# Encoder trunk on one core: four blocks of weight splits moved from VectorE to GpSimd, and the work around them put in another order

## The reference, cut to what matters

```python
def reference(x, ...):                       # x: (1, 1024, 1024), DEPTH = 2, all float32
    for l in range(DEPTH):
        h = rms_norm(x, norm_mix_g[l])
        proj = h @ w_in[l]                   # columns q, k, v (512 each), z_b (512), x_c (256)
        q, k, v, z_b, x_c = jnp.split(proj, splits, axis=-1)
        mix_a = neighbourhood_attention(q, k, v, rpb[l])       # 8 heads of 64, 8 x 16 neighbours
        mix_b = spatial_gating(z_b, ...)                       # gelu, layer norm, 128 x 128 per head
        mix_c = fourier_mix(x_c)                               # real part of a 2-D DFT per group
        mix = head_rms_norm(jnp.concatenate([mix_a, mix_b, mix_c], axis=-1), head_norm_g[l])
        x = x + mix @ w_out[l]
        h = rms_norm(x, norm_ffn_g[l])
        x = x + (jax.nn.silu(h @ w_gate[l]) * (h @ w_up[l])) @ w_down[l]
    return rms_norm(x, final_norm_g)
```

## Time and profile before

| | |
|---|---|
| runs, us | 2043.91, 2045.06, 2043.42 (median 2043.91) |
| profiled execution, us | 2043.91 |
| its span, us | 2042.1 |
| TensorE busy | 2007.0 us, 98% of the span |
| VectorE busy | 1537.9 us, 75% |
| ScalarE busy | 902.5 us, 44% |
| GpSimd busy | 208.9 us, 10% |
| mean granted clock of TensorE | 0.997 |

### The profile page before, as it was taken

The page is one execution under the profiler, slowest core; times in us unless marked ns, Lnnn a source line. Parts: engine busy times, 40 slices in busy tenths (PEclk is TensorE's granted clock), DMA queues, the critical chain, the costliest instruction groups (busy, mean ns, idle before and its releaser), DMA issues.

```text
span 2042.1 us, 28134 instructions
## 1 busy us (share of the span) xinstructions
PE 2007.0 (98%) x10156; PEld 1670.0 (82%) x10156; DVE 1537.9 (75%) x2519; ACT 902.5 (44%) x1611; POOL 208.9 (10%) x146
## 2 busy tenths in 40 slices
PE   7999899999999999999999999999999999999998
PEld 7888688888888888888898877888888888888887
DVE  7847874789877778787867488647997877878877
ACT  6453773443333333444644547634433333334443
POOL 1221133200000000000013022431000000000000
PEclk9999999999999999999999999999999999999999
DMA  6965754124333236633468667441343333383333
GB/s 236 216 165 139 230 155 140 51 93 166 125 111 106 98 111 253 200 99 97 121 193 206 160 176 234 133 133 42 102 172 130 109 100 102 109 322 105 95 97 124
DMA packets 131560, 293.70 MB, mean 144 GB/s; under 512 B 13024, under 2 KB 18016, under 8 KB 131168
## 3 DMA queue, kind: packets, MB, share of 16 engines
q1 hardware_dynamic: 105760, 242.63, 36.3%
q0 software_dynamic: 10880, 20.97, 6.1%
q10 hardware_dynamic: 14784, 28.31, 3.8%
HBM read 232.62 MB, written 59.24 MB: 143 GB/s over the span
## 4 chain that ended last, share of the span: by engine, by line
PE 90%; DVE 6%; issue 2%; ACT 1%; ACTq 0%; DMA 0%; POOL 0%; DVEq 0%
PE bank L2184 27%; PE bank L2185 27%; PE bank L2186 27%; PE bank L2386 2%; PE bank L2405 2%; PE bank L2335 2%; DVE s_lo L1429 1%; DVE t_lo L1848 0%; PE bank L2298 0%; PE bank L2427 0%; PE bank L2314 0%; PE bank L2420 0%; ACT s_hi L953 0%; ACT logits L1149 0%; DVE h_lo L1755 0%
## 5 line engine op out<-in xcount | busy, mean ns | idle before, releaser
L2184 PE MATMUL bank<-t_hi,s_hi 128*128 128x512 f32 (+1 forms) x1336 | 517.7, 388 | 0.7 <-DVE hid_cu L1961 0.4
L2185 PE MATMUL bank<-t_lo,s_hi 128*128 128x512 f32 (+1 forms) x1336 | 517.1, 387 | 0.0
L2186 PE MATMUL bank<-t_hi,s_lo 128*128 128x512 f32 (+1 forms) x1336 | 517.1, 387 | 0.0
L2184 PEld LDWEIGHTS bank<-t_hi,s_hi 128*128 128x128 f32 x1336 | 251.1, 188 | 52.4 <-DVE hid_cu L1961 1.3
L2186 PEld LDWEIGHTS bank<-t_hi,s_lo 128*128 128x128 f32 x1336 | 251.1, 188 | 50.6
L2185 PEld LDWEIGHTS bank<-t_lo,s_hi 128*128 128x128 f32 x1336 | 251.1, 188 | 50.5
L2184 PE MATMUL bank<-b_hi,s_hi 128*128 128x512 f32 x528 | 206.3, 391 | 0.1
L2186 PE MATMUL bank<-b_hi,s_lo 128*128 128x512 f32 x528 | 205.8, 390 | 0.0
L2185 PE MATMUL bank<-b_lo,s_hi 128*128 128x512 f32 x528 | 205.7, 390 | 0.0
L953 ACT ACTIVATE s_hi<-w_u 128x512 fp32r<-128x512 f32 x142 | 89.6, 631 | 233.1 <-PE bank L2186 175.8
L953 ACT ACTIVATE s_hi<-w_down 128x512 fp32r<-128x512 f32 x154 | 97.3, 632 | 200.2 <-PE bank L2186 199.3
(11 more groups left out here) (291 smaller groups left out, 3749.6 us busy)
## 6 DMA issues: line engine op xcount, KB each, us to landing
w_raw<-in_win SPq DMA_DIRECT2D x50, 512.0 KB, 6.0
w_g<-in_wg SPq DMA_DIRECT2D x44, 512.0 KB, 3.5
w_u<-in_wu SPq DMA_DIRECT2D x44, 512.0 KB, 4.4
t_raw<-hidden_t SPq DMA_DIRECT2D x88, 256.0 KB, 2.6
w_raw<-in_win POOLq DMA_DIRECT2D x40, 512.0 KB, 7.2
bias<-in_bias SPq DMA_DIRECT2D x24, 768.0 KB, 5.0
t_raw<-hidden_b SPq DMA_DIRECT2D x66, 256.0 KB, 2.6
hidden_b<-hid_g SPq DMA_DIRECT2D x60, 256.0 KB, 2.0
```

Of the source, the lines that this page charges most:

```text
L2184: nc.tensor.matmul(bank, lh, rh, start=start, stop=False, skip_group_check=reopened)
L2185: nc.tensor.matmul(bank, lh, rl, start=False, stop=False, skip_group_check=reopened)
L2186: return nc.tensor.matmul(bank, ll, rh, start=False, stop=stop, skip_group_check=reopened)
```

## The change

- `block_lo` of products 2 to 5 (eight pieces per layer) leaves VectorE. GpSimd makes these low parts (`blocks_lo`, `piece_lo`), in one queue with the accumulating DMAs that it issues. The wait of SyncE before `store_sum(5)` goes.
- TensorE: the position DFT comes ahead of product 2 and the channel DFT between its banks 1 and 2.
- VectorE: the 13 DFT steps come before the low parts of operand b11; the differences, low parts and taps of the stretch after it are interleaved.
- ScalarE: the copies of the channel DFT come before operand `n2` and the high parts of product 4; `piece_hi` of product 3's second piece comes before the last two banks of tap 1.
- Start of attention: ScalarE makes the high parts of the even q blocks right after `probs(1)`. VectorE runs `head_norm(1)` ahead of `logits(0)`, `head_scale(1)` right after `tap(13, 3)`, and `query_rest(0, c)` ahead of `logits(2)`.

```diff
 (SyncE)
                 load_blocks(l, 6, 2)
-                sp.wait_ge(w_ready, split_nth(l, piece(4, 1)))
                 store_sum(l, 5)
 (GpSimd)
+            def blocks_lo(l, *products):
+                for n in products:
+                    for i in range(2):
+                        if n in IN_THIRDS:
+                            pool.wait_ge(s2_stored, 64 * l + 32 * (IN_THIRDS.index(n) + 1))
+                        piece_lo(l, piece(n, i))
...
+                pool.wait_ge(w_ready, split_nth(l, piece(1, 1)))
+                blocks_lo(l, 2)
                 add_term(l, 4, 1)
+                piece_lo(l, piece(3, 0))
                 add_term(l, 4, 2)
+                piece_lo(l, piece(3, 1))
                 add_term(l, 5, 1)
+                blocks_lo(l, 4)
                 add_term(l, 5, 2)
                 add_term(l, 6, 1)
+                blocks_lo(l, 5)
                 pool.wait_ge(hs_var, l * 2 + 1)
                 nc.gpsimd.tensor_tensor(SR[:, :], SS[:, :], NHALF[:, :], ALU.pow).then_inc(hs_rstd, 1)
 (ScalarE)
                 tap(0)
-                tap(1)
+                tap(1, 0, 1)
+                piece_hi(l, piece(3, 1))
+                tap(1, 2, 3)
...
-                piece_hi(l, piece(3, 1))
-                blocks_hi(l, 4)
-                operand("n2")
                 act.wait_ge(dft_full, l * 8 + 8)
...                                            (copies of the channel DFT)
+                operand("n2")
+                blocks_hi(l, 4)
                 act.wait_ge(mc_made, l * 4 + 4)
                 nc.scalar.activation(SQB[1][:, :, :], MC, ACT.Square).then_inc(hs_sq, 1)
                 blocks_hi(l, 5)
...
                 probs(0)
                 probs(1)
+                for c in range(4):
+                    wait_tapped(act, l, 13, c)
+                    nc.scalar.activation(q_view(QH, 2 * c), q_view(QR_, 2 * c), ACT.Copy).then_inc(qk_hi, 1)
 (VectorE)
-                        dve.wait_ge(w_ready, split_nth(l, 1))
-                        if n in IN_THIRDS:
-                            dve.wait_ge(s2_stored, 64 * l + 32 * (IN_THIRDS.index(n) + 1))
+                        dve.wait_ge(w_ready, split_nth(l, piece(5, 1) if n > 5 else 1))
...
-                for k in range(4):
-                    operand_low("b11", k)
-                block_lo(2)
...                                            (the 13 DFT steps)
+                for k in range(4):
+                    operand_low("b11", k)
...                                            (norms)
+                differences(0)
...                                            (copies of the position DFT)
+                for k in range(1, 4):
+                    differences(k)
+                    operand_low("n2", k - 1)
+                    tap(2, k - 1)
+                operand_low("n2", 3)
+                tap(2, 3)
                 for k in range(4):
-                    differences(k)
-                block_lo(3)
-                for k in range(4):
-                    operand_low("n2", k)
-                block_lo(4)
-                tap(2)
...
-                block_lo(5)
+                    later_differences(k)
+                tap(3)
...
                 tap(13, 2)
+                head_norm(1, MB, SQB[0][:, :, :])
...
                 logits(0)
                 logits(1)
                 tap(13, 3)
-                head_norm(1, MB, SQB[0][:, :, :])
+                head_scale(1, MB)
...
                     if i:
                         logits(2 * i)
                         logits(2 * i + 1)
+                    else:
+                        for c in range(4):
+                            query_rest(0, c)
...
-                    if i == 2:
-                        for c in range(4):
-                            query_rest(0, c)
-                        head_scale(1, MB)
 (TensorE)
                 in_product(1)
-                in_bank(2, 0)
-                in_bank(2, 1)
...
                 position_dft(0, (4, 5, 6))
                 position_dft(1, (7, 4, 5))
-                in_bank(2, 2)
-                in_bank(2, 3)
+                in_bank(2, 0)
+                in_bank(2, 1)
...
                 channel_dft(0)
                 channel_dft(1)
+                in_bank(2, 2)
+                in_bank(2, 3)
```

More of the change, by code:

```diff
@@ L1194, in _ @@
                         probs(2 * i + 1)
-                    if i == 1:
-                        for c in range(4):
-                            wait_tapped(act, l, 13, c)
-                            nc.scalar.activation(q_view(QH, 2 * c), q_view(QR_, 2 * c), ACT.Copy).then_inc(qk_hi, 1)
                     for n in {0: (0, 1), 7: ()}.get(i, (i + 1,)):
```

## The result

| | before | after |
|---|---|---|
| runs, us | 2043.91, 2045.06, 2043.42, 2042.78 | 2077.36, 2074.49, 2078.06, 2075.79 |
| median, us | 2043.66 | 2076.57 |
| profiled execution / span, us | 2043.91 / 2042.1 | 2076.69 / 2074.7 |
| mean granted clock of TensorE | 0.997 | 0.990 |

The changed kernel takes 1.016 times as long (95% interval 1.0142 to 1.0177), 32.9 us more. The forecast was 2058 with a range up to 2068, so the direction was right and the size was missed by 18 us.

A forecast was written before the change was run, and what follows sets the result against it. TensorE, busy 98% of the span, was taken as the bound, so any late input becomes time. 7.8 (product 5) + 4.0 (attention) + 2.6 (low clock) = +14.4 on 2043.91 gave 2058.3 us, range 2047 to 2068.

The forecast's parts named there:

- The new chain to product 5: Input projection, GpSimd's queue to product 5's low parts: TensorE waits 4.7 us, net 3.9 a layer, 7.8 in all.
- the low parts of products 2 and 3: GpSimd's queue in the projection: they end 12 us or more before they are due, costed at nothing.
- Product 4 is in time, by 1 to 3 us: Projection: GpSimd's low parts end at 94.3, product 4 due at 95.72, its second piece 1.36 later.
- The DFTs: Projection on TensorE: position DFT directly after product 1, product 3 starting at 84.84; gain 0.84 us a layer.
- The 0.84 us ahead of product 3: TensorE's wait for the channel DFT's copies in the projection, claimed to go: gain 0.84 us a layer.
- Its input is ready: Position DFT in the projection: the 13 steps moved ahead on VectorE let it start at 62.40.
- The start of attention: VectorE stands 4 us at the scaling, TensorE 8 us before scores(2): +2.0 a layer, 4.0, plus 2.6 for clock.
- a new low clock in layer two: After TensorE's 8 us stand at the start of attention, the low clock comes in layer two also: +2.6 us.
- Rival 3: GpSimd's low parts slower beside VectorE, at double time 4.8 us, four a layer on the chain: 2077; chance 0.03.
- Rival 2: Chain to product 5 longer, by stores near 7.6 us or a low clock after each wait: 2068; chance 0.20.

The follow-up runs named there:

- Experiment 3: The changed kernel with the low parts of products 2 to 5 back on VectorE and SyncE's wait ahead of store_sum(5) restored: 2050.92 us (1.0031).
- experiment 5: The changed kernel with only the low parts of products 2 and 3 on GpSimd, those of 4 and 5 on VectorE: 2064.10 us (1.0099).
- experiment 6: The changed kernel with only the low parts of products 4 and 5 on GpSimd, those of 2 and 3 on VectorE: 2064.79 us (1.0102).
- experiment 10: Kernel before with the attention edits except the early head_scale(1), plus DFT steps first and TensorE's new order; low parts on VectorE: 2037.41 us (0.9965).
- experiment 11: Kernel before with only head_norm(1) moved in attention, plus DFT steps first and TensorE's new order; low parts on VectorE: 2037.44 us (0.9966).

## Why the prediction was wrong, step by step

**The step that failed** stands in "The new chain to product 5": "the low parts of products 2 and 3 end 12 us or more before they are due, so I cost them at nothing". I looked at when GpSimd's result is due, and it was early, as said: product 2's low parts ended at 58.25, and the product started at 76.32. The cost was on VectorE, whose DFT steps beside it take 2.6 us instead of 0.42. Experiments 3 and 5 size it: the low parts of products 2 and 3 cost 13.2 us, and in the sum this term was zero. Those of products 4 and 5 cost 13.9 (experiment 6); 3.4 of that are TensorE's waits for GpSimd's low part, the chain that the forecast had, and the rest it had not. All eight together cost 25.7.

**"Product 4 is in time, by 1 to 3 us"** failed for the same reason and for one more. I followed only the weights' low parts. Product 4 also needs the banks of product 3's tap, and tap 3 now stood behind all eight later differences on VectorE. Experiment 3, without any hold from GpSimd, still shows 2.1 us a layer there; the hold makes it 3.8. VectorE's queue was never costed up to tap 3.

**Product 5's chain** was sized right, or too short, and mattered less. The added terms landed 5.9 and 7.3 us after their issue (8.1 taken for the second), the store 7.8 us after it (4.3 taken), and the low part came at 121.4 where 110.3 was forecast. But product 5 itself was due at 120.45, 13.9 us later than forecast, so 1.7 us a layer showed and not 4.7. The delays upstream hid it. So 3.9 us a layer for this chain is not shown by the changed kernel, and experiment 6, in which only this chain and the differences are slowed, has the same 1.7.

**The DFTs.** The 0.84 us ahead of product 3 went, as forecast, and experiments 10 and 11 point to it as a gain where nothing holds VectorE. "Its input is ready", at a start forecast for 62.40, failed: product 1 was done at 63.02 and the steps at 63.86.

**The start of attention** was right in its numbers: 3.98, 8.1 and 214.62 us against 4, 8 and 215.2, with the low clock in both layers. Its price came to 4.0 us alone and 4.4 inside the change, of 6.6 forecast. By layer the changed kernel's stretches behind the projection grew by 0.9 and 3.5 us, where 2.0 and 4.6 were forecast. They are 2.5 us apart, and the 2.6 for a new low clock in layer two alone is just that; so what was taken too high, by about 1.1 us, is common to both layers. No run here separates it further.

**The rivals.** Rival 3 names 2077, close to the measured 2076.6, and had a chance of 0.03. Its time is a coincidence of sizes: it put the cost on the chain to product 5. It said that GpSimd's low parts would take double; they took 2.4 us as before where VectorE was the one to stand (the longest of 50 took 4.1), and the time went to VectorE. Its hint was the right one. The Trainium skill ("SBUF — State Buffer", section "Who interferes with whom") says that a VectorE instruction with two SBUF inputs and a GpSimd instruction that reads SBUF exclude each other for the whole instruction, and that one with at most one SBUF input, outside the modes that use both of VectorE's ports, is not touched. The traces agree: 2.63 us for 0.42 with two SBUF inputs, 0.68 us beside a 2.37 us low part with one input from PSUM. Rival 2's long store came too (7.8 us), but was hidden. Had I read the duration of VectorE's instructions beside GpSimd's (the pair at 1011 us), the price of a low part would have been about 2 us on VectorE, more than the 1.2 us that it saves there.

**What stays open.** One VectorE instruction took 5.06 us (from 58.46, and one of nearly the same length stands in layer two), through two DMA issues of GpSimd and the whole low part behind them. Turns don't explain it: GpSimd was issuing DMAs when it began, and such issues held none of the differences from 103.22 on. And about 2.9 us of the projection's 27.7 have no row. I did not try other splits of the work between the engines, such as low parts on GpSimd only where VectorE works out of PSUM.

## What to carry to other kernels

Before moving work from VectorE to GpSimd, look up in the trace how long VectorE's instructions take beside a GpSimd instruction of that kind, and cost the move by what stands in VectorE's queue there, not by when GpSimd's result is due: with two SBUF inputs on VectorE, a subtraction of 2.4 us on GpSimd took about 2 us of VectorE's time to save 1.2. When a helper chain is moved earlier (here the head norm), leave its consumer where it was, if it stands in one queue with work that is needed sooner: the early scaling cost 9 us, and without it the same move gained 5.

## What the hardware showed that I had not expected

- Where VectorE's instructions have two SBUF inputs, VectorE and GpSimd take turns of whole instructions: 128x256 in 2.63 instead of 0.42 us, 128x512 in 2.47 to 2.88 instead of 0.68, and with GpSimd's instructions halved 1.78, in step with GpSimd's 1.74.
- One input on GpSimd's side is enough: beside a copy of 1.2 us (two of them in 2.33) the 0.42 us step took 1.26.
- GpSimd stands as well, in some places: its low part, 2.4 us in the median of 50, took 3.34 us at 59.89 and 3.89 at 69.89, beside VectorE's instructions with two SBUF inputs. At 69.89 it stood about 1.5 us through VectorE's norms of 0.68 each, so the turns don't always alternate one by one.
